# Expert stage of a diffusion trunk: gathers of U of the next head and of V of this head in turn, routing two heads ahead, loops unrolled

## What is computed

```python
qry = (xb @ wq).reshape(n, 8, 2, 64)                      # 8 heads, two halves
s1 = einsum('nhd,hkd->nhk', qry[:, :, 0], sub_keys[:, 0]) # 128 keys per half
s2 = einsum('nhd,hkd->nhk', qry[:, :, 1], sub_keys[:, 1])
v1, i1 = top_k(s1, 16);  v2, i2 = top_k(s2, 16)
cand = v1[..., :, None] + v2[..., None, :]                # 256 candidates
sc, pos = top_k(cand.reshape(n, 8, 256), 16)
idx = take_along_axis(i1 * 128 + i2 (all pairs), pos)     # 16 experts per token and head
g = softmax(sc)
act = gelu(einsum('nd,nhkd->nhk', xb, peer_u[idx]))       # 16 rows of U per token and head
y = einsum('nhk,nhkd->nd', g * act, peer_v[idx])          # 16 rows of V
```

## Time and profile before

| | |
|---|---|
| median of the timed runs (3) | 5119.65 us |
| lowest and highest | 5118.15, 5122.17 us |
| span of the profiled execution | 5121.3 us |
| PE busy | 3764.5 us (74%) |
| DVE busy | 2862.3 us (56%) |
| POOL busy | 2687.4 us (52%) |
| ACT busy | 1063.2 us (21%) |
| gathers' queue: packets, MB, share of 16 DMA engines | 368640, 1342.34, 69.8% |

### The profile page before, as it was taken

The page is one execution under the profiler, slowest core; times in us unless marked ns, Lnnn a source line. Parts: engine busy times, 40 slices in busy tenths (PEclk is TensorE's granted clock), DMA queues, the critical chain, the costliest instruction groups (busy, mean ns, idle before and its releaser), DMA issues.

```text
span 5121.3 us, 48248 instructions
## 1 busy us (share of the span) xinstructions
PE 3764.5 (74%) x12022; PEld 1932.4 (38%) x12034; DVE 2862.3 (56%) x6385; ACT 1063.2 (21%) x2469; POOL 2687.4 (52%) x2761
## 2 busy tenths in 40 slices
PE   7897867676767767676668978666766676677666
PEld 3465533333333333333324555333333333333332
DVE  2524455656565565656645363566666656666664
ACT  1123111221121121122121241112212221222221
POOL 2700045565566565666656300566666666666665
PEclk8998688888888888888889977888888888888888
DMA  5122269999999999999981102799999999999998
GB/s 172 31 76 83 75 238 339 358 343 352 344 356 356 344 361 335 358 348 358 364 334 39 47 2 75 269 366 362 349 358 366 363 355 361 366 356 359 355 367 312
DMA packets 512066, 1453.42 MB, mean 284 GB/s; under 512 B 52896, under 2 KB 171108, under 8 KB 511844
## 3 DMA queue, kind: packets, MB, share of 16 engines
q0 software_dynamic: 368640, 1342.34, 69.8%
q1 hardware_dynamic: 143336, 109.91, 6.8%
HBM read 1448.83 MB, written 3.24 MB: 284 GB/s over the span
## 4 chain that ended last, share of the span: by engine, by line
PE 41%; DMA 21%; issue 20%; POOL 9%; DVE 6%; ACT 2%; POOLq 1%; SPq 0%; DVEq 0%; ACTq 0%
PE ps L536 39%; DMA arena<-in_peer_u,rows_for_u 21%; POOL arena L519 6%; POOL arena L527 3%; DVE arena L1362 1%; PE ps L640 1%; DVE arena L1283 1%; ACT arena L1072 1%; POOLq L517 0%; DVE expert_weight L1369 0%; ACT expert_gelu L1058 0%; DVE arena L1266 0%; DVE arena L1296 0%; DVE gate_rec L1367 0%; DVE arena L1171 0%
## 5 line engine op out<-in xcount | busy, mean ns | idle before, releaser
L536 PE MATMUL ps<-arena 128*128 128x512 f32 (+7 forms) x9648 | 3407.6, 518 | 1189.5 <-ACT arena L1072 1140.9
L536 PEld LDWEIGHTS ps<-arena 128*128 128x128 f32 (+3 forms) x9648 | 1701.3, 206 | 2825.9 <-issue 1553.0
L1362 DVE CUSTOM_DVE_ANT_0 arena<-arena,ps 128x1024 f32<-128x1024 f32 x1280 | 1562.9, 1221 | 1321.4 <-DMA arena<-in_peer_u,rows_for_u 1272.4
L527 POOL DMA_INDIRECT arena<-in_peer_v,rows_for_v x1280 | 1214.1, 948 | 1028.1 <-PE ps L536 806.5
L519 POOL DMA_INDIRECT arena<-in_peer_u,rows_for_u x1280 | 1200.1, 938 | 583.1 <-issue 429.6
L1072 ACT ACTIVATE arena<-constants,expert_weight 128x128 f32<-128x128 f32 x1280 | 475.5, 396 | 953.0 <-PE ps L536 892.8
L1058 ACT ACTIVATE expert_gelu<-expert_act 128x16 f32<-128x16 f32 x80 | 17.3, 216 | 1264.7 <-DVE expert_act L1362 1264.7
L1211 DVE TENSOR_REDUCE score_max<-ps 128x1 f32<-128x640 f32 (+1 forms) x80 | 57.4, 718 | 302.9 <-PE ps L536 302.9
L504 POOL MEMSET arena<- 128x5632 f32 x2 | 9.6, 4792 | 405.7 <-ACTq L258 405.7
L536 PE MATMUL ps<-arena,cond_silu 128*2 128x128 f32 (+1 forms) x1344 | 186.7, 294 | 19.2 <-DMA arena<-in_ada_w 11.9
L497 POOL TENSOR_SCALAR arena<-arena,vec_columns 128x512 f32<-128x512 f32 x120 | 153.0, 1286 | 10.5 <-issue 10.5
(11 more groups left out here) (163 smaller groups left out, 1894.5 us busy)
## 6 DMA issues: line engine op xcount, KB each, us to landing
arena<-in_ada_w SPq DMA_DIRECT2D x80, 512.0 KB
arena<-in_peer_u,rows_for_u POOLq DMA_INDIRECT x1280, 6.5
arena<-in_peer_v,rows_for_v POOLq DMA_INDIRECT x1280, 6.1
arena<-in_w_in SPq DMA_DIRECT2D x32, 512.0 KB, 4.0
arena<-in_ada_w SPq DMA_DIRECT2D x4, 2048.0 KB, 17.1
arena<-in_w_out SPq DMA_DIRECT2D x4, 2048.0 KB, 7.7
arena<-in_peer_wq SPq DMA_DIRECT2D x2, 4096.0 KB, 18.1
peer_modulation<-modulation_rows SPq DMA_DIRECT2D x4, 1536.0 KB, 11.2
```

The costliest lines, as they stand in the source:

```text
L527: pool.indirect_dma_start(VR[:, k % RING, :], None, v_rows, bass.IndirectOffsetOnAxis(ap=idx_v[:, k:k + 1], axis=0))\
L536: return pe.matmul(out, lhsT, rhs, start=start, stop=stop)
L1362: dve.tensor_tensor_reduce(out=UR[:, k % RING, :], in0=UR[:, k % RING, :], in1=pair(1), scale=1.0, scalar=0.0, op0=ALU.mult, op1=ALU.add, ...
```

## The change

- POOL asks for the U rows of head 0 first, and then for U row k of head g+1 and V row k of head g in turn. The expert numbers of four heads are kept (`rows`, `LIVE = 4`), so the copy `idx_v` falls away; the gate's Exp and its sum are kept for four heads too.
- `route` of head g+2 stands inside the dots of head g, ahead of k = 8, instead of behind them.
- PE and ACT compute the query and scores three heads ahead of the V rows (k = 0 and 5 on PE; k = 2, 7 and, for the Exp, 13 on ACT). The query is computed in transposed form, so the separate transpose and its copy fall away.
- The GELU of head g+1 comes at the end of ACT's loop for head g.
- The accumulator is opened and closed by the first and last product of a tile; the products with zeros are gone. `tile_transposes` stands ahead of head 5 of a tile. `normed` of the next tile follows the second head's dots and `residual` of the last tile those of the third.
- The loops over heads are unrolled, waits are on constants, and the `sem_inc` of `pool_turn` and `dve_turn` are gone.

```diff
@@ POOL @@
-                with pool.Fori(0, NT * HEADS) as i:
-                    head = NT * HEADS * l + i
-                    pool.wait_ge(S["idx_ready"], head + 1)
...
+                def gather_u(g, k):
+                    n = T * l + g
+                    if k == 0:
+                        pool.wait_ge(S["idx_ready"], n + 1)
+                    if n * TOPK + k >= RING:
+                        pool.wait_ge(S["u_free"], n * TOPK + k + 1 - RING)
+                    pool.indirect_dma_start(UR[:, k % RING, :], None, u_rows,
+                                            bass.IndirectOffsetOnAxis(ap=rows[:, g % LIVE, k:k + 1], axis=0))\
+                        .then_inc(u_in[k % RING], 16)
...
+                for k in range(TOPK):
+                    gather_u(0, k)
+                for g in range(T):
                     for k in range(TOPK):
+                        if g + 1 < T:
+                            gather_u(g + 1, k)
+                        gather_v(g, k)
@@ PE @@
+                for g in range(T):
+                    t, h, n = g // HEADS, g % HEADS, T * l + g
+                    if h == 0 and NT * l + t:
+                        pe.wait_ge(S["acc_out"], NT * l + t)
+                    if h == HEADS - 3 and t + 1 < NT:
                         tile_transposes(l, t + 1)
+                    for k in range(TOPK):
...
+                        if g + 3 < T:
+                            if k == 0:
+                                query(l, g + 3)
+                            if k == 5:
+                                key_scores(l, g + 3)
+                        pe.wait_ge(v_in[k % RING], n * 32 + 16 * (k // RING + 1))
+                        pe.wait_ge(S["diag_ready"], n * TOPK + k + 1)
@@ ACT @@
+            def gate_exp(l, g):
+                n = T * l + g
+                act.wait_ge(S["idx_ready"], n + 1)
+                if n >= LIVE:
+                    act.wait_ge(S["w_ready"], n - LIVE + 1)
+                act.activation(gexp[:, g % LIVE, :], centred[:, :], ACT.Exp,
+                               accum_out=gsum[:, g % LIVE:g % LIVE + 1]).then_inc(S["exp_done"], 1)
...
+                        if n * TOPK + k >= DIAGS:
+                            act.wait_ge(S["v_free"], n * TOPK + k + 1 - DIAGS)
...
+                    if g + 1 < T:
+                        expert_gelu(l, g + 1)
@@ DVE @@
+            def head_dots(l, g):
+
+                n = T * l + g
                 for k in range(TOPK):
-                    if k == 9:
-
-                        dve.wait_ge(S["v_free"], head * TOPK + RING)
-                        dve.tensor_copy(idx_v[:, :], idx_u[:, :]).then_inc(S["idxv_ready"], 1)
-                    dve.wait_ge(u_in[k % RING], head * 32 + 16 * (k // RING + 1))
+                    if k == 8 and g + 2 < T:
+                        route(l, g + 2)
+                    dve.wait_ge(u_in[k % RING], n * 32 + 16 * (k // RING + 1))
...
+                dve.wait_ge(S["exp_done"], n + 1)
+                dve.reciprocal(grec[:, :], gsum[:, g % LIVE:g % LIVE + 1])
+                dve.wait_ge(S["gelu_done"], n + 1)
...
             def peer(l):
+                route(l, 1)
+                for g in range(T):
```

More of the change, by code:

```diff
@@ L32 @@
 DIAGS = 4
+LIVE = 4
+T = 40
 C_ID, C_MEAN, C_ROT, C_DUP, C_MASK, C_COS, C_SIN, C_SCAN, C_IOTA, C_ONE = (
@@ L830, in out_project @@
-                key_scores(g + 1, 1)
+                key_scores(l, 1)
                 mix(4, 1)
[L833 to L852, removed]
@@ L854, in peer @@
             def peer(l):
                 pe.wait_ge(S["res_read"], NT * (l + 1))
[L856 to L867, removed]
-                        tile_transposes(l, t + 1)
[L869 to L876, removed]
+                query(l, 2)
@@ L1050, in scores_out @@
+            def scores_out(l, g):
+                n = T * l + g
+                act.wait_ge(S["sc_ps"], n + 1)
+                if n:
+                    act.wait_ge(S["sc_taken"], n)
                 act.activation(SCC[:, :, :].rearrange("p a b -> p (a b)"), PS[:, 4, 0:256], ACT.Copy)\
                     .then_inc(S["sc_now"], 1)
[L1053 to L1073 removed]
@@ L1318, in top16, with route @@
                 dve.max_index(inds[:, 8:16], vals[:, 8:16], spare)
-            def route(l, head):
-                dve.wait_ge(S["sc_now"], head + 1)
-                dve.sem_inc(S["dve_turn"], 1)
+            def route(l, g):
+                n = T * l + g
+                dve.wait_ge(S["sc_now"], n + 1)
                 for s in range(2):
@@ L1332, in route @@
                 top16(best[:, :], pos[:, :], CAND, CAND2)
+                if n:
+                    dve.wait_ge(S["exp_done"], n)
                 dve.drain()
@@ L1399, in out_project @@
                 gated_residual(2)
-                route(l, HEADS * NT * l)
+                route(l, 0)
                 for t in (3, 4):
@@ L1405, in peer @@
             def peer(l):
-                if l == 0:
-                    dve.sem_inc(S["u_free"], RING)
-                for t in range(NT):
-                    n = NT * l + t
-                    dve.drain()
-                    dve.tensor_copy(pair(1), H2[:, t % 2, :])
-                    if t + 1 < NT:
-                        normed(l, t + 1)
-                    dve.drain()
-                    with dve.Fori(0, HEADS if t + 1 < NT else HEADS - 1) as i:
-                        head_dots(HEADS * n + i)
-                        route(l, HEADS * n + 1 + i)
-                        dve.drain()
-                    if t + 1 == NT:
-                        head_dots(HEADS * n + HEADS - 1)
-                    if t:
+                route(l, 1)
+                for g in range(T):
+                    t, h = g // HEADS, g % HEADS
+                    if h == 0:
+                        dve.drain()
+                        dve.tensor_copy(pair(1), H2[:, t % 2, :])
+                        dve.drain()
+                    head_dots(l, g)
+                    if h == 1 and t + 1 < NT:
+                        normed(l, t + 1)
+                    if h == 2 and t:
                         residual(l, t - 1)
```

181 lines of the change are left out of this document (82 added, 99 removed).

## The result

| | before | after |
|---|---|---|
| median of the timed runs, us (4 each) | 5118.9 | 4721.66 |
| lowest and highest | 5115.52, 5122.17 | 4721.26, 4724.11 |
| ratio to before, with its 95% interval | | 0.9224 [0.9211, 0.9237] |
| span of the profiled execution, us | 5121.3 | 4722.3 |

The forecast was 4658 us (4590 to 4830). The time lies in the range, in rival A's own range too (4600 to 4740), and 64 us above the forecast.

The account below looks back on a forecast made before the run. The prediction took a loop through several engines, with saturated and starved DMA halves, as the bound; DMA would bind after. Savings of 219.5 us in layer 1 and 242.7 in layer 0 gave span 4659.1, forecast 4658 us, range 4590 to 4830.

Parts of the forecast that it names:

- rival A: Expert stages: DMA-bound as summed, own range 4600 to 4740 us; chance 0.72.
- starved half: Part of each head before: 263 GB/s, POOL starting a gather each 1.71 us because V slots wait for PE.
- slabs: Layer 0's expert stage: 48 modulation loads of 524 KB at 1.67 us each, 80 us on the DMA.
- Start and end of the stages: Each expert stage: 34.4 us from first gather to U(1,0); last GELU 8.3 us after 39 rounds; PE's end 2 us less.
- 32 x 1.277 = 40.87 us of DMA per head: Expert stages: DMA serves 32 gathers per head at 1.277 us each, 40.87 us against 46.84 in layer 1 before.
- full half: Part of each head before: DMA saturated at 410 to 412 GB/s, POOL starting a gather each 1.24 us.
- Can the ring hide the route?: Ring of 8 slots, route before dot 8: 10.2 us left for landing against 7.1 measured, margin 3 us, cost nothing.
- Rival C: Margin of 3 us missing, DMA runs dry at each route: from 3 us per head, 4890 us; chance 0.09.
- B: Expert stages: POOL's gather pitch binds and slabs are free, 175 us less: 4480 us; chance 0.03.
- D: DMA's mean rate cannot pass 358 GB/s: period 46.9 us, 5118 us, no change; chance 0.03.
- E: POOL's gathers get longer beside the route: at + 0.57 us each, 4920 us; chance 0.08.
- F: PE works at 1.2 GHz, a head takes 59.6 us: slower than before, above 6200 us; chance 0.03.

Follow-up runs that it names:

- e4b: The changed kernel with query and scores at k = 0 on PE and POOL's order put back to 16 U rows, then 16 V rows: 5077.83 us.
- e4c: The changed kernel with query and key scores both at k = 0 on PE, ACT's copies at k = 0 and 1: 4715.26 us.
- e6: The kernel before with gathers of 2 KB half rows instead of 4 KB: 4911.58 us.
- e2: The changed kernel with one eighth of each of layer 0's 48 modulation slabs loaded, PE's work kept: 4644.02 us.
- e1: The changed kernel with the route cut into three parts, ahead of dots 7, 9 and 11: 4707.37 us.
- e8: The changed kernel with one reduction in the route done seven times, making the route 4.6 us longer: 4775.33 us.
- e10: The changed kernel with 16,000 empty instructions on SP during layer 1's expert stage: 4718.09 us.
- e5: The changed kernel with gathers of 2 KB half rows instead of 4 KB: 4529.66 us.
- e3: The kernel before with only the loops over heads of POOL, PE, ACT and DVE unrolled: 5134.89 us, ratio 1.0033.

## Why the prediction was right, and where it was off

**The mechanism** held: rival A. V no longer stands in front of U in POOL's order, the starved half is gone, and the DMA is in work all the time. e4b against e4c shows that nine tenths of the gain go when the turns are taken out of the changed kernel; e6 shows that the kernel before had no bound of bytes. Not shown is what the turns would bring to the kernel before by themselves.

**Where the 63 us of span are** (4722.3 against 4659.1):
- Layer 1's period 41.56 against 40.87: 39 x 0.69 = 27 us.
- Layer 0's period 43.76 against (1593.9 + 80.2 + 3.8)/39 = 43.02: 29 us. The same gathers give 27 of it and the slabs 48 x 0.08 = 4 (1.75 us each by e2 against 1.67), 2 more than there are.
- Layer 0's stage began 10.5 us later (695.1 against 684.6), in code that the change does not touch. The forecast had nothing for that.
- Start and end of the stages: -3 us. From the first gather to U(1,0) 33.9 us against 34.4, the first GELU at 41.3.

**The term that was mis-sized** is 32 x 1.277 = 40.87 us of DMA per head; it measured 41.56. The 1.277 us of a gather came from 20 us of the full half. In the first 360 us of layer 1's stage the profile gives 408 GB/s, 0.5243 MB / 408 = 1.285 us; over 3080 to 4660 the mean is 406.0, or 1.291 us. The period gives 41.56/32 = 1.299, mostly because not all of the 406 are gathers. What the short full halves of before could not show are dips like those at 3727. I looked at the single packets in the DMA records of the trace: a packet of 4 KB takes 160 ns in the median, and a gather's 128 packets over 16 engines are eight each, 1.28 us, about the least that it can take. Between 3100 and 4600 (before: 3300 to 5060) a few take longer than 250 ns, most of them 300 to 600:

| kernel | median landing, us | packets over 250 ns | their excess over 160 ns, us in 1000, over 16 engines |
|---|---|---|---|
| e1 | 16.6 | 0.34% | 6.6 |
| after | 10.8 | 0.46% | 9.9 |
| e8 | 6.8 | 1.1% | 23 |
| before | 6.4 | 3.1% | 60 |

Within the kernel after, the first 360 us have an excess of 4.0 in 1000 and the rest 11.8, and the rate falls from 408 to 405 with it. An estimate from these records closes the 0.69 us per head: 32 x 1.28 instead of 1.277 is 0.10, the slow packets 9.9 in 1000 are 0.41, the stores of the results of four tiles (0.524 MB each, 4 x 1.28 us in 39 heads) are 0.13, and the instruction fetches, 1.77 us in 1000, are 0.07; together 0.71. The forecast had the last three at nothing. It is an estimate, since the records' own times overlap (their sum is a share of 1.02).

The excess falls as the queue gets deeper, but e1 shows that a queue of 16.6 us does not remove it. Only e8 and e1 change the depth by a single edit; the kernel before differs in much else. What makes these packets slow stays open. e10 was to test the fetches and did not raise them. By time, 17% of the slow packets of the kernel after lie beside a recorded fetch, where 4% would by chance; so fetches may have a part, but at most a sixth of it.

**Can the ring hide the route?** The arithmetic held, its reading did not. Landing may take 10.2 us before dot 8 holds POOL; I put 7.1 there and 8 to 10 for after, and called the rest margin. But POOL asks each 1.245 us and the DMA serves each 1.28 to 1.30, so the queue grows until something stops it, and what stops it is that hold. Landing goes to the limit and 1 us past it (11.3 us at 3715), and the hold takes the 41.56 - 32 x 1.245 = 1.7 us per head by which POOL is faster. The margin is always used up, and costs nothing as long as it is queue. e8 moves the limit down by 4.6 us and the median landing follows it by 4.0. Rival C was the right mechanism for a longer route, with a milder price: it had 3 us a head, e8 cost 0.74 in layer 1 and 0.24 in layer 0.

**The other rivals.** B: POOL's pitch is the next bound, and near: 40.2 us (e5) against 41.56; but with rows of 4 KB the slabs are not free. In e5, where the DMA has slack, they are: 40.20 in layer 0, 40.22 in layer 1. D: refuted, 406 GB/s over 1400 us. The Trainium skill, "DMA: Bandwidth & Descriptors", section "Where 436 GB/s comes from", has about 358 GB/s as the limit from HBM, and works it out as one of two cores' part of 716 GB/s. These gathers, in a program on one core, pass it by 13%; no run here has the other core at work. E: the effect is there, and small. In layer 1's stage 49 of 1280 gathers lasted over 1.0 us (1.2 in the mean), and 44 of these 49 lie beside a route, where only 332 of the 1280 do. What they take beyond the usual 0.94 is 12 us in all, 0.3 a head, and hidden, since POOL waits more than that; lengths of both lines in 3200 to 4600, in ns:

```profile
L519 POOL DMA_INDIRECT arena<-in_peer_v,expert_rows x539: 936/941/1165, 3199.3 to 4598.7; - x180
```

```profile
L511 POOL DMA_INDIRECT arena<-in_peer_u,expert_rows x539: 935/941/1937, 3200.5 to 4599.9; - x180
```

F: the clock stayed at 1.00; PE takes up a V row each 2.55 us and waits 0.58 of them. PE's timeline after:

```profile
3788.12 1.98 PE L536 MATMUL ps<-arena 128*128 128x512 f32 x4 [0.58 <-DMA arena<-in_peer_v,expert_rows]
3790.68 1.98 PE L536 MATMUL ps<-arena 128*128 128x512 f32 x4 [0.58 <-DMA arena<-in_peer_v,expert_rows]
3793.23 1.98 PE L536 MATMUL ps<-arena 128*128 128x512 f32 x4 [0.56 <-DMA arena<-in_peer_v,expert_rows]
```

**Costed at nothing.** Unrolling is a loss of 0.33% alone (e3), 17 us; no run has the changed kernel with its loops, so there it is not known. The route on DVE: its length is about as before (10.4 us in the median, 10.2 before), and the dots behind it catch up at 1.14 us each, faster than the 1.28 that I used. DVE's timeline after: the last dot ahead of the route, the route's first and last row, and two dots.

```profile
3331.41 1.22 DVE L1351 CUSTOM_DVE_ANT_0 arena<-arena,ps 128x1024 f32<-128x1024 f32 x1 [1.32 <-DMA arena<-in_peer_u,expert_rows]
...
3332.56 0.29 DVE L1296 MAX8 top_values<-arena 128x8 f32<-128x128 f32 x1
...
3342.92 0.23 DVE L1341 TENSOR_SCALAR expert_rows<-chosen_expert 128x16 uint32<-128x16 f32 x1
3343.07 1.21 DVE L1351 CUSTOM_DVE_ANT_0 arena<-arena,ps 128x1024 f32<-128x1024 f32 x1
...
3344.21 1.21 DVE L1351 CUSTOM_DVE_ANT_0 arena<-arena,ps 128x1024 f32<-128x1024 f32 x1
```

## What to carry to other kernels

A DMA share of 0.95 is not a bound: read the rate in short windows, and if full and starved stretches alternate, look for the queue in which a transfer without a free slot stands in front of one that has one. Two streams with users of different pace belong in turn on such a queue, and the work that feeds the second (here the scores) must not stand behind the first's last rows. When the queue is full, its landing time grows to whatever the ring allows, so forecast the hold from the difference of the two paces and not from today's landing time; and take the service time over hundreds of us, or leave one or two per cent for slow packets.

## What the runs showed of the hardware

- Gathers of 128 rows of 4 KB from one queue kept a core at 406 GB/s for 1400 us (128 packets of 160 ns over 16 engines for each), with rows of 2 KB at 210 GB/s: there POOL is the limit, at 1.25 us a gather for either size (e5).
- A load of 512 KB in pieces of 512 bytes costs 1.75 us of a full DMA (e2), a gather of the same bytes 1.28 to 1.30.
- Where fewer gathers were queued, more packets were slow (0.34% in e1, 0.46% after, 1.1% in e8, 3.1% before). A DMA share near 1 can go with 355 GB/s: 0.97 at 3727 to 3730 in the kernel after.
- Gathers get longer beside a route on VectorE: 44 of the 49 over 1.0 us in layer 1's stage, 1.2 us instead of 0.94.
